# Mixed order for the expert blocks behind the fixed eight, weights requested by first use

## The reference, cut to what matters

```python
lg = xt @ rg_w + rg_b                       # 4 groups: take the best one
le_sel = logits of the 8 experts of that group
v2, e_idx = lax.top_k(le_sel, 2)            # two experts per token, of 32
w2 = softmax(v2) * p_top
act = silu(xt @ w_gate[e]) * (xt @ w_up[e]) * gate    # 1024 -> 128, per chosen expert
out = act @ w_down[e]                                 # 128 -> 1024
```

## Time and profile before

| | |
|---|---|
| median of 3 runs | 608.03 us (608.02 to 610.11) |
| the profiled execution | 608.55 us |
| its span | 606.5 us |
| PE busy | 571.4 us, 94% of the span |
| DVE, ACT, POOL busy | 439.9, 242.2, 88.5 us |
| DMA | 111.27 MB, mean 183 GB/s over the span |
| granted TensorE clock, mean | 0.981 of full speed |

### The profile page before, as it was taken

How to read it: one execution, slowest core, us unless ns; L and a number is a source line. 1 busy time by engine, 2 the same in 40 slices (tenths; PEclk the granted TensorE clock), 3 DMA queues, 4 the chain that set the end, 5 groups by cost and what they waited for, 6 DMA issues and landing times.

```text
span 606.5 us, 9765 instructions
## 1 busy us (share of the span) xinstructions
PE 571.4 (94%) x3401; PEld 473.4 (78%) x3401; DVE 439.9 (73%) x749; ACT 242.2 (40%) x389; POOL 88.5 (15%) x136
## 2 busy tenths in 40 slices
PE   8899999999999999899999995899997999999775
PEld 6799999997899889688888874777654768887222
DVE  4937997999999696746666658899731667786285
ACT  6642112222212427322222116576322567775443
POOL 4300000200000000100000000433331334431000
PEclk9999999999999999999999997899998999999889
DMA  8761210131112202455422107699989999962697
GB/s 317 150 123 38 69 36 1 36 93 35 36 36 79 105 36 69 114 203 198 157 80 93 54 36 247 215 332 404 392 329 412 407 352 395 394 241 97 209 421 299
DMA packets 52598, 111.27 MB, mean 183 GB/s; under 512 B 10867, under 2 KB 29176, under 8 KB 51449
## 3 DMA queue, kind: packets, MB, share of 16 engines
q1 hardware_dynamic: 44773, 92.18, 43.2%
q0 software_dynamic: 7168, 17.84, 8.2%
q10 hardware_dynamic: 596, 0.50, 0.3%
HBM read 96.36 MB, written 21.86 MB: 195 GB/s over the span
## 4 chain that ended last, share of the span: by engine, by line
PE 51%; DVE 17%; DMA 7%; issue 3%; ACT 2%; SPq 1%; POOL 0%; POOLq 0%; DVEq 0%; ACTq 0%
PE ps L2259 14%; PE ps L2081 9%; PE ps L2425 6%; PE ps L2364 3%; PE ps L2386 3%; PE ps L2400 3%; PE ps L2401 3%; PE ps L2402 3%; DMA at_opair_p<-scratch_out 3%; DMA at_wlater<-in_expert_w_down 3%; DVE at_mixP L1360 3%; PE ps L2496 2%; PE ps L2323 2%; DVE at_hT L1319 1%; DVE at_lnsq L1546 1%
## 5 line engine op out<-in xcount | busy, mean ns | idle before, releaser
L2081 PE MATMUL ps<-at_hT,at_ring 128*128 128x384 f32 x936 | 165.5, 333 | 0.0
L2081 PEld LDWEIGHTS ps<-at_hT,at_ring 128*128 128x128 f32 x936 | 155.9, 188 | 5.1 <-issue 5.0
L2259 PE MATMUL ps<-at_hT,at_mring 128*128 128x512 f32 (+1 forms) x432 | 102.7, 393 | 2.0 <-DVE at_mring L1514 1.3
L2259 PEld LDWEIGHTS ps<-at_hT,at_mring 128*128 128x128 f32 (+1 forms) x432 | 77.3, 182 | 21.3 <-DVE at_mring L1514 1.7
L1360 DVE SCALAR_TENSOR_TENSOR at_mixP<-at_uc,at_par,at_mixP 128x1024 f32<-128x1024 f32 x60 | 77.1, 1285 | 2.1
L2400 PE MATMUL ps<-at_whi,at_hTm 128*128 128x256 f32 x176 | 51.0, 290 | 0.0
L2402 PE MATMUL ps<-at_whi,at_hTm_lo 128*128 128x256 f32 x176 | 49.1, 279 | 0.0
L2364 PEld LDWEIGHTS ps<-sb_ident,at_xg 128*128 128x128 f32 x232 | 29.3, 192 | 18.2 <-issue 15.2
L1795 DVE TENSOR_TENSOR at_wlater_lo<-at_wlater,at_whi 128x1024 fp32r<-128x1024 f32 x30 | 36.7, 1225 | 6.0 <-ACT at_whi L988 5.1
L2425 PE MATMUL ps<-at_wlater,at_actT 128*128 128x512 f32 (+1 forms) x92 | 38.0, 597 | 0.7 <-ACT at_actT L1003 0.7
L988 ACT ACTIVATE at_whi<-at_wlater 128x1024 fp32r<-128x1024 f32 x30 | 31.6, 1055 | 7.3 <-PE ps L2402 6.5
(11 more groups left out here) (324 smaller groups left out, 919.2 us busy)
## 6 DMA issues: line engine op xcount, KB each, us to landing
at_wlater<-in_expert_w_gate SPq DMA_DIRECT2D x20, 512.0 KB, 11.1
at_wlater<-in_expert_w_up SPq DMA_DIRECT2D x20, 512.0 KB, 12.8
at_wlater<-in_expert_w_down SPq DMA_DIRECT2D x20, 512.0 KB, 15.4
at_raw<-in_w_in SPq DMA_DIRECT2D x16, 512.0 KB, 4.0
at_opair_p<-scratch_out SPq DMA_DIRECT2D x8, 1024.0 KB, 14.7
at_wfirst<-in_expert_w_gate SPq DMA_DIRECT2D x12, 512.0 KB, 9.0
at_wfirst<-in_expert_w_up SPq DMA_DIRECT2D x12, 512.0 KB, 10.0
at_wfirst<-in_expert_w_down SPq DMA_DIRECT2D x12, 512.0 KB, 12.5
```

What stands on the lines that cost most here:

```text
L2081: mm = pe.matmul(ps[:, bank + r, 0:t1 - t0], w[:, wpart, k * P:(k + 1) * P], hT[:, hpart, k, t0:t1], start=(m, wpart, hpart) == (0, 0, 0), ...
L2259: mm = pe.matmul(ps[0:n, b + r, :], mring[:, 1 - i % 2, mpart, k * P:k * P + n], wo[:, wpart, k, r * 512:(r + 1) * 512], start=(c, mpart, ...
```

## The change

The order of the 21 blocks behind the fixed eight becomes a string, and every function reads a table that is made from it. The new order is X L P M X L L L M M P M P P M M M M M P M: the same two X, four L, five P and ten M. The list LOADS says in which order the 24 experts are loaded: by first use in that order. Load w now belongs to position LOADS[w - 8], and `experts(r)` gives the loads of block r. The wait on the last use of load w-8 stands as it was, with the new table behind it. A class of four tiny experts per block (QUADS) is added to the code, but with QUADS = 0 none of its instructions is issued. The counters `iox` are written by two more iotas.

```diff
-FIX, PAIRS, LARGE = 8, 5, 4
+FIX, PAIRS, QUADS, LARGE, EXTRA = 8, 5, 0, 4, 2
+TINY = 4 * QUADS
+LIGHT = TINY + 2 * PAIRS
+LANES = LARGE // EXTRA
+NB = FIX + PAIRS + QUADS + EXTRA + LARGE + MID
+ORDER = "XLPMXLLLMMPMPPMMMMMPM"
+
+def table():
+    first = {"Q": 0, "P": TINY, "X": LIGHT, "L": LIGHT, "M": LIGHT + LARGE}
+    count = {"Q": 4, "P": 2, "X": LANES, "L": 1, "M": 1}
+    out = []
+    for k in ORDER:
+        out.append((k, list(range(first[k], first[k] + count[k]))))
+        first[k] += count[k]
+    return out
+
+TABLE = table()
+LOADS = list(dict.fromkeys(c for _, cs in TABLE for c in cs))
...
+def experts(r):
+    if r < FIX:
+        return [r]
+    if r >= NB:
+        return [r + NE - NB]
+    return [FIX + LOADS.index(c) for c in TABLE[r - FIX][1]]
 def is_pair(r):
-    return FIX <= r < X0 or X0 <= r < M0 and (r - X0) % 3 == 0
+    return len(experts(r)) > 1
...
 def done_in(w):
-    return max(r for r in range(NB + LAP) if w in ([place(r, 0), place(r, 1)] if is_pair(r) else [place(r)]))
+    return max(r for r in range(NB + LAP) if w in experts(r))
...
             for w in range(FIX, NE):
-                e = sp.value_load(eid[0:1, w - FIX:w - FIX + 1], min_val=0, max_val=NE - 1)
+                c = LOADS[w - FIX]
+                e = sp.value_load(eid[0:1, c:c + 1], min_val=0, max_val=NE - 1)
                 sp.wait_ge(s["d_done"], done_in(w - LAP) + 1)
                 load_expert(0, w, e, False)
...
             for h in range(2):
-                do(g.iota(iox[h * 64:h * 64 + 64, :], [[2, PAIRS + EXTRA]], base=h, channel_multiplier=0, **flt))
+                do(g.iota(iox[h * 64:h * 64 + 64, 0:PAIRS], [[2, PAIRS]], base=TINY + h, channel_multiplier=0, **flt))
+            for n0, n, first, lanes in ((PAIRS, QUADS, 0, 4), (PAIRS + QUADS, EXTRA, LIGHT, LANES)):
+                for t in range(lanes if n else 0):
+                    q = slice(t * P // lanes, (t + 1) * P // lanes)
+                    do(g.iota(iox[q, n0:n0 + n], [[lanes, n]], base=first + t, channel_multiplier=0, **flt))
```

More of the change, by code:

```diff
@@ L42 @@
 TCOLS = NE * CAPB
-FIX, PAIRS, LARGE = 8, 5, 4
+FIX, PAIRS, QUADS, LARGE, EXTRA = 8, 5, 0, 4, 2
 REST = NE - FIX
-LIGHT = 2 * PAIRS
-EXTRA = LARGE // 2
-NB = NE - PAIRS + EXTRA
+TINY = 4 * QUADS
+LIGHT = TINY + 2 * PAIRS
 MID = REST - LIGHT - LARGE
-X0 = FIX + PAIRS
-M0 = X0 + 3 * EXTRA
+LANES = LARGE // EXTRA
[11 more added lines that the diff above has]
+LOADS = list(dict.fromkeys(c for _, cs in TABLE for c in cs))
 OVER = 19
@@ L119, in __call__, with lane @@
         self.eng.wait_ge(sem, self.n[key])
+def experts(r):
[4 more added lines that the diff above has]
+    return [FIX + LOADS.index(c) for c in TABLE[r - FIX][1]]
 def is_pair(r):
-    return FIX <= r < X0 or X0 <= r < M0 and (r - X0) % 3 == 0
+    return len(experts(r)) > 1
 def place(r, t=0):
[L129 to L136, removed]
+    return experts(r)[t]
+def lane(r, t):
+    n = P // len(experts(r))
+    return slice(n * t, n * t + n)
 def done_in(w):
-    return max(r for r in range(NB + LAP) if w in ([place(r, 0), place(r, 1)] if is_pair(r) else [place(r)]))
+    return max(r for r in range(NB + LAP) if w in experts(r))
 def split(i, r):
@@ L149, in column @@
 def column(r):
[L151 to L156, removed]
+    k, cs = TABLE[r - FIX]
+    if k == "P":
+        return (cs[0] - TINY) // 2
+    if k == "Q":
+        return PAIRS + cs[0] // 4
+    if k == "X":
+        return PAIRS + QUADS + (cs[0] - LIGHT) // LANES
+    return PAIRS + QUADS + EXTRA + cs[0] - LIGHT
 def rows(i):
@@ L311, in build_layer @@
         iob = sb("iob", [1, OVER])
-        iox = sb("iox", [P, PAIRS + EXTRA])
+        iox = sb("iox", [P, PAIRS + QUADS + EXTRA])
         pid = sb("pid", [P, TILES, 2])
@@ L1675, in _, with running @@
             rest = carry[:, FIX:NE]
-            s_left, l_all, l_left, l_from = (left[:, n:n + 1] for n in range(4))
+            s_left, q_left, p_from, l_from = (left[:, n:n + 1] for n in range(4))
+            tiny, quads = (which[:, n * REST:(n + 1) * REST] for n in range(2))
+            def running():
+                do(v.tensor_tensor_scan(run, ones[:, 0:REST], few, 0.0, ALU.mult, ALU.add))
             def class_experts():
-                do(ts(few, rest, 64.0, None, ALU.is_le))
-                do(v.tensor_tensor_scan(run, ones[:, 0:REST], few, 0.0, ALU.mult, ALU.add))
-                do(stt(small, run, LIGHT + 0.5, few, ALU.is_le, ALU.mult))
-                do(ts(taken, run, float(LIGHT), None, ALU.min))
+                if QUADS:
+                    do(ts(few, rest, 32.0, None, ALU.is_le))
+                    running()
+                    do(stt(tiny, run, TINY + 0.5, few, ALU.is_le, ALU.mult))
+                    do(ts(quads, run, float(TINY), None, ALU.min))
+                do(ts(few, rest, 64.0, None, ALU.is_le))
+                if QUADS:
+                    do(tt(few, few, tiny, ALU.subtract))
+                running()
+                do(stt(small, run, 2 * PAIRS + 0.5, few, ALU.is_le, ALU.mult))
+                do(ts(taken, run, 2.0 * PAIRS, None, ALU.min))
                 do(ts(few, rest, float(P), None, ALU.is_gt))
-                do(v.tensor_tensor_scan(run, ones[:, 0:REST], few, 0.0, ALU.mult, ALU.add))
+                running()
             def place_experts():
@@ L1702, in place_experts @@
                 do(tt(held, held, few, ALU.mult))
+                if QUADS:
+                    do(stt(quads, quads, -1.0, mid, ALU.add, ALU.subtract))
+                    do(tt(quads, quads, tiny, ALU.mult))
+                    do(tt(held, held, quads, ALU.add))
                 do(tt(mid, mid, late, ALU.add))
@@ L1843, in columns, with lane_columns, quad_columns @@
                 return tab[:].rearrange("p (e c) -> p e c", c=CAPB)[:, FIX:NE, c]
-            def pair_columns(c, at_, count):
-                do(v.tensor_copy(late[0:64, :], columns(c)[0:64]))
-                do(v.tensor_copy(late[64:P, :], columns(c)[0:64]))
+            def lane_columns(c, at_, count, lanes):
+                n = P // lanes
+                for t in range(lanes):
+                    do(v.tensor_copy(late[t * n:t * n + n, :], columns(c)[0:n]))
                 pick(iox, at_, at_, count, late)
             def light_columns():
-                pair_columns(0, 0, PAIRS)
+                lane_columns(0, 0, PAIRS, 2)
+            def quad_columns():
+                if QUADS:
+                    lane_columns(0, PAIRS, QUADS, 4)
             def extra_columns():
-                pair_columns(1, PAIRS, EXTRA)
+                quad_columns()
+                lane_columns(1, PAIRS + QUADS, EXTRA, LANES)
             def other_columns():
-                pick(io32, LIGHT, PAIRS + EXTRA, LARGE + MID, columns(0))
+                pick(io32, LIGHT, PAIRS + QUADS + EXTRA, LARGE + MID, columns(0))
                 do(v.tensor_copy(sperm[:], pcols[:]))
@@ L1874, in overflow_counts @@
                 do(stt(again[:, FIX:NE], rest[0:1, :], 64.0, few[0:1, :], ALU.is_gt, ALU.mult))
+                if QUADS:
+                    do(ts(few[0:1, :], pos[0:1, :], TINY - 0.5, None, ALU.is_le))
+                    do(stt(few[0:1, :], rest[0:1, :], 32.0, few[0:1, :], ALU.is_gt, ALU.mult))
+                    do(tt(again[:, FIX:NE], again[:, FIX:NE], few[0:1, :], ALU.max))
                 do(ts(few[0:1, :], pos[0:1, :], LIGHT + LARGE - 0.5, -1.0, ALU.is_ge, ALU.add))
-                do(stt(run[0:1, :], rest[0:1, :], P + 64.5, few[0:1, :], ALU.is_le, ALU.mult))
+                do(stt(run[0:1, :], rest[0:1, :], P + P // LANES + 0.5, few[0:1, :], ALU.is_le, ALU.mult))
                 do(stt(few[0:1, :], pos[0:1, :], LIGHT - 0.5, run[0:1, :], ALU.is_ge, ALU.mult))
@@ L2379, in expert_GU @@
                     pe.wait_ge(s["htm_hi"], b + 1)
-                    for t in range(2):
-                        w = place(j, t)
+                    for w in experts(j):
                         pe.wait_ge(w_in_sem[w % LAP], 48 * lap(i, w) + 48)
                     for k in range(KC):
-                        for t in range(2):
-                            n = slice(64 * t, 64 * t + 64)
+                        for t, w in enumerate(experts(j)):
+                            n = lane(j, t)
                             mm = pe.matmul(out[n], hTp[:, j % 2, k, n],
-                                           half(wexp(place(j, t)), k // 4)[:, :, k % 4, :],
+                                           half(wexp(w), k // 4)[:, :, k % 4, :],
                                            start=k == 0, stop=k == KC - 1)
@@ L2422, in expert_D @@
                     q = 2 * D + r * 512
-                    for t in range(2) if is_pair(j) else (None,):
-                        n = slice(0, P) if t is None else slice(64 * t, 64 * t + 64)
+                    for t, w in enumerate(experts(j)):
+                        n = lane(j, t)
                         mm = pe.matmul(ps[n, bank + r, :], actT[:, j % 2, n],
```

(2 more changed lines are left out.)

17 lines of the change are left out of this document (13 added, 4 removed).

## The result

The changed kernel is slower: 621.18 us median of 4 runs (619.99 to 622.2) against 609.07 (608.02 to 610.69) for the kernel before, run beside it; the ratio is 1.0202, 95% interval 1.018 to 1.0224. The forecast was 616.5 us, +8.5, and a range of 608 to 623; the time lies in the upper part of the range and the difference of the medians is +12.1.

What follows compares the result with a forecast made beforehand. Bound: PE, with DMA close behind. Four loads behind the gap put w31 at 559.8, plus 2.9 for the split: block 28 +8.5 us; 608.55 + 8.5 = 617.1, less 0.5 for the median, 616.5 us; range 608 to 623.

Steps and rivals of the forecast that it cites:

- 7.0 us of slack at w31: Old order's end: last load w31 lands at 544.3, ScalarE starts splitting the last block's weights at 551.28.
- w16 waits for block 9, w17 for block 13: SP load queue: w17 issued at 473.3 instead of 446.9, 26 us later, with w18 to w31 behind it.
- The price of four loads: Load stream behind the gap: four loads behind, 5.98 MB at 386 GB/s, 15.5 us, so w31 lands at 559.8.
- the start from an empty queue: First load after the gap, w17: extra time between 0 and 6.6 us, taken as nothing.
- The signs: What would show the forecast right: empty load queue 451 to 473, w31 landing 557 to 563, tail as long as before.
- Slots do not delay w31: End of the load stream: w31 waits for block 21, which ends at 515, by 525 with waits in front.
- At no cost: Lone pairs cost 0.9 us of PE, hidden by weight waits; placing code unchanged; two iotas covered, 0.4 us otherwise.
- A: Rival, expert stage: DMA serves the backlog at the fast pace, 5.20 us per load or faster, down to 604.2 us; chance 0.08.
- B: Rival, expert stage: comes out even, pace 5.2 to 5.4 or thin DMA recovered, 608 to 611 us; chance 0.12.
- E: Rival, load stream: slow pace of 6.46 us per load with split matmuls waiting, 624 to 626 us; chance 0.08.
- D: Rival, PE in blocks 19 to 28: slow clock paid after each weight wait, 3 x 1.4 us, 620.8 us; chance 0.10.
- T3: Experiments' suspicion, expert stage's start: something else in the edit, since block 8 began 2.1 us later in the changed kernel's profile.

Runs made afterwards that it cites:

- e1: Changed kernel with only the old order string put back, all other edits kept: 609.6 us, ratio 0.9981 to the kernel before.
- e11: Changed kernel's code with the old order, load w22 made to wait for block 14 instead of 11: 614.71 us, ratio 1.0089 to the kernel before.
- e2: Changed kernel, new order kept, each load put into the slot that comes free first instead of w modulo 8: 610.12 us, ratio 0.9991 to the kernel before.
- e3: Changed kernel with one letter moved, the first extra pair's second large block at 10 instead of 13: 610.32 us, ratio 0.9994 to the kernel before.
- e4: Changed kernel with the first two loads exchanged, so w16 already waits for block 13: 623.7 us, ratio 1.0223 to the kernel before.
- e5: Changed kernel's code with the old order, load w22 made to wait for block 16 instead of 11: 620.28 us, ratio 1.016 to the kernel before.
- e9: Changed kernel run once more, unchanged, beside the kernel before: 620.17 us, ratio 1.0179.
- e7: Changed kernel with another order, PXLLPXLLPMPMPMMMMMMMM, slots still w modulo 8: 605.0 us, ratio 0.9899 to the kernel before.

## Why the prediction was right, and where its size was off

- *The order is bound by PE with DMA close behind; 7.0 us of slack at w31.* Held as to DMA close behind, but 7.0 is the number of one execution: in e1, the old order again, w31 landed at 542.8 and block 28 started at 556.2, which is 10.5 us of slack. e11 cost less than its loads were late, so there is slack; how much at w31 it does not measure, since w29 was the load that held it up.
- *Gain of 4.7 us at blocks 12 and 13.* Held: no wait for weights up to block 18, in both profiles of the changed kernel; but the gain was more than given back.
- *w16 waits for block 9, w17 for block 13, with w18 to w31 behind it.* Held to the instruction; e2, e3 and e4 each move this wait by a different edit, and the time follows in all three. The forecast for w17's issue was 473.3; it was 476.0 in one profile and 474.5 in the other. Of the 2.7, 2.1 came from block 8's start. My sentence that a block ends as the transposes of block j+2 begin was wrong: it is j+3. The sum had used j+3 (block 16 for block 13), so its numbers stood; the expectation of e5 did not.
- *DMA at about 100 GB/s in the gap.* 100 GB/s. The price of four loads, 15.5 us at 386 GB/s: the pace behind it came out at 5.81 us per load in the sum and at 5.80 in the profile (5.81 in e9). The stretches within it were less even than the sum had them, 405, 384 and at the end 273 GB/s.
- *The terms that were too small: the start from an empty queue, and the time of the issue.* I gave the start's bounds as 0 and 6.6 us and took 0, and the first load at 478.5. It landed at 483.4: 2.7 us from the later issue, and 2.2 from the start, since it landed 7.4 us behind its first issue instead of 5.2. In e9 it is 1.2 from the issue and 2.1 from the start (7.3 behind the issue); together 3.3, and w31 was 563.2 - 559.8 = 3.4 late. That is the difference between +8.5 and the +11.8 us of block 28 in e9 (566.0 against 554.2). In the first profile block 28 was 13.2 late, of which 2.1 were block 8's.
- *The signs.* w31 was to land at 557 to 563; it landed at 564.6 and 563.2, both outside. The tail behind block 28 was to be as long as before, 52.3 us; it was 50.7 and 50.5, which hid part of the miss. That is the execution again: e1, with the old order, has 50.6, and the profiles range from 49.7 to 52.3.
- *Slots do not delay w31, block 21 ends by 525.* Wrong as it stands: w30 and w31 wait for block 21, and w30 was issued at 533.05, as that block ended; the profile's chain runs through this wait. DMA was full then (1.03 from 530 to 550), so whether an earlier issue would have brought w31 forward is not shown.
- *2.9 us from w31 to block 28.* 2.8 in both profiles.
- *At no cost: iotas, placing code, lone pairs.* e1 for the code; some 0.6 us for the pairs (estimated 0.9), hidden.

The rivals. A and B (DMA catches up) fell with the pace of 5.80, where 5.20 was needed, and so did E with its 6.46. D, the slow clock that adds up: it did fall behind two of the five waits, and the paired matmuls of blocks 20 and 27 took 5.3 us instead of 3.6.

```profile
509.24 5.27 PE L2451 MATMUL ps<-at_wlater,at_hTp 128*64 128x256 f32 x32 [3.09 <-DMA at_wlater<-in_expert_w_down]
...
559.50 5.36 PE L2451 MATMUL ps<-at_wlater,at_hTp 128*64 128x256 f32 x32 [3.13 <-DMA at_wlater<-in_expert_w_down]
```

In the window from 509 to 512 the granted clock was 0.52, so nearly all at 1.2 GHz. But block 28 started 2.8 us behind w31's landing although block 27 had been slow: the lost time lay inside the next wait, as argued. What was argued for the last wait came true as well: where a slow block had no wait for weights behind it, it was paid, 1.3 us in e11 (block 26) and 1.5 in e4 (block 28's matmuls took 4.6 us instead of 3.1, at a clock of 0.63). The Trainium skill's account (TensorE: Matmul & The Clock Gate, section HAM oscillation — how this bites in real kernels) agrees as to the cold matmuls behind waits; that they are paid for each time did not hold in the changed kernel, where the next wait was for DMA again.

## What to carry to other kernels

Where loads are issued in a fixed order by one queue, and each waits for its slot, the wait that matters is the last use of the longest-held slot: everything behind it stands too, free slots or not. A gap there shows no stall where it arises (PE was fully busy for those 15 us); count the bytes behind it, compare their time with the slack of the last load, and add a few us for the restart. Here mixing heavy and light blocks did harm where the use of a shared load was stretched over the mix: with one large block three places late it cost 2%. With each extra pair followed at once by its two large blocks the loss was gone, but that alone brought nothing (e3, ratio 0.9994, with a pair as the last block but one); e7, with the middle blocks last, brought 1%. Which of its differences from e3 made the gain was not tested one by one.

## What the runs showed of the hardware that I had not expected

- A load of 1.5 MB into an empty queue took 7.3, 7.4, 7.7 and 9.8 us from first issue to landing (e9, the changed kernel, e4, e11), though its bytes alone are 3.9 us at 386 GB/s. It does not need loads right behind it for that: w16 of the changed kernel also met an empty queue (w15 had landed at 448.7), had no load behind it for 23.7 us, and took 7.3 as well, 452.33 to 453.23 + 6.4 = 459.6. Gathers and scatters ran beside it, and DMA moved 284 GB/s. What a load takes with nothing at all beside it no run shows. Why e11's took 9.8 is open.

```profile
at_wfirst<-in_expert_w_down SPq DMA_DIRECT2D x1, 512.0 KB, 6.4
```

```profile
452.30:459.60 7.30, 7.30 (x56) 5.41 (x56) 3.29 (x9) 2.84 (x6) 2.32 (x3) 1.00 0.89 284
```

- The clock at the start of the expert stage differs between executions whose work up to there is the same: from 388 to 394 it was 1.00 in the kernel before and 0.72 in e7, and block 0's matmuls took 3.1 or 4.3 us. Block 8 started between 432.2 and 434.8 in the profiles, with no pattern by order (e1 433.1, e9 432.7, e7 434.8); the changed kernel itself has 434.3 and 432.7 (e9). So T3's 2.1 us are an execution's, not the edit's.
